# Eight query heads in place of zero-padded ones: 64-row score matmuls in one attention branch

## The reference

```python
C_HEADS, C_KV_HEADS, HEAD_DIM = 8, 2, 64          # branch C: 8 query heads share 2 key/value heads
D_HEADS, D_NOPE, D_ROPE, D_V = 8, 64, 32, 64      # branch D: 8 heads, keys of 64 + 32

def block_attention(q, k, v, scale):              # q (b, l, kv heads, heads per kv head, dk)
    ...
        s = jnp.einsum('bqhgd,bkhd->bhgqk', qblk, k, preferred_element_type=jnp.float32) * scale
        p = jax.nn.softmax(s, axis=-1).astype(v.dtype)
        return jnp.einsum('bhgqk,bkhd->bqhgd', p, v)

def cd_attend(qc, qd, kc, vc, kd, vd, w_out):
    oc = block_attention(qc, kc, vc, HEAD_DIM ** -0.5)
    od = block_attention(qd, kd, vd, (D_NOPE + D_ROPE) ** -0.5)
    return jnp.concatenate([oc, od], axis=-1) @ w_out
```

## Time and profile before

| what | value |
|---|---|
| time, median of 3 runs | 1847.87 us (1847.65 to 1848.35) |
| the profiled execution's own time | 1847.87 us |
| its span in the trace | 1845.5 us |
| mean granted TensorE clock | 0.955 of full speed |
| PE, PEld, DVE, ACT busy | 92%, 76%, 75%, 50% of the span |
| POOL busy | 2.1 us in 6 instructions |
| DMA | 426.38 MB, mean 231 GB/s |

### The profile page before, as it was taken

One profiled execution on the slowest core, in us unless ns is written; L12 is line 12 of the kernel. 1 busy time (PEld: TensorE's weight loads), 2 busy tenths in 40 slices (PEclk: granted clock), 3 DMA queues, 4 the chain that ended last, 5 costly groups with the idle time before them and its releaser, 6 DMA issues.

```text
span 1845.5 us, 22486 instructions
## 1 busy us (share of the span) xinstructions
PE 1693.2 (92%) x8417; PEld 1393.4 (76%) x8418; DVE 1390.7 (75%) x1444; ACT 920.0 (50%) x844; POOL 2.1 (0%) x6
## 2 busy tenths in 40 slices
PE   4988899999999796897799999999899999999995
PEld 1876777888887595566688877888788887888884
DVE  5858757777787827673698977888698977888886
ACT  5421232221221424332577776777677676777773
POOL 0000000000000000000000000000000000000000
PEclk9988999999999798898799999999999999999998
DMA  9543334543675232001499998999899998999992
GB/s 352 190 152 128 117 106 135 178 147 132 208 236 195 64 115 69 23 1 40 141 348 336 360 339 294 347 343 358 279 357 332 359 334 285 352 342 358 336 365 91
DMA packets 214552, 426.38 MB, mean 231 GB/s; under 512 B 8186, under 2 KB 64028, under 8 KB 214452
## 3 DMA queue, kind: packets, MB, share of 16 engines
q1 hardware_dynamic: 210218, 420.37, 65.4%
q10 hardware_dynamic: 4234, 4.57, 0.8%
HBM read 423.86 MB, written 1.05 MB: 230 GB/s over the span
## 4 chain that ended last, share of the span: by engine, by line
PE 87%; DVE 6%; ACT 2%; issue 2%; DMA 1%; SPq 1%; DVEq 0%; ACTq 0%
PE bank L505 26%; PE bank L507 25%; PE bank L506 25%; PE bank L1751 2%; PE bank L1806 2%; DVE lo L464 2%; PE bank L1740 2%; PE bank L1845 1%; PE bank L1526 1%; DMA raw<-in_ada_w_dram 1%; PE bank L1757 1%; PE bank L1520 1%; ACT hi L458 1%; PE bank L1879 0%; PE bank L1880 0%
## 5 line engine op out<-in xcount | busy, mean ns | idle before, releaser
L464 DVE TENSOR_TENSOR lo<-raw,hi 128x2048 fp32r<-128x2048 f32 x361 | 820.7, 2282 | 225.9 <-ACT hi L458 224.2
L458 ACT ACTIVATE hi<-raw 128x2048 fp32r<-128x2048 f32 x361 | 689.1, 1911 | 492.6 <-PE bank L507 471.9
L505 PE MATMUL bank<-hi,xgh 128*128 128x512 f32 (+1 forms) x864 | 331.3, 383 | 24.6 <-issue 18.3
L506 PE MATMUL bank<-lo,xgh 128*128 128x512 f32 (+1 forms) x864 | 327.9, 380 | 0.0
L507 PE MATMUL bank<-hi,xgl 128*128 128x512 f32 (+1 forms) x864 | 327.5, 379 | 0.0
L506 PEld LDWEIGHTS bank<-lo,xgh 128*128 128x128 f32 x864 | 164.4, 190 | 46.7 <-issue 15.0
L505 PEld LDWEIGHTS bank<-hi,xgh 128*128 128x128 f32 x864 | 164.5, 190 | 42.5 <-DVE lo L464 6.5
L507 PEld LDWEIGHTS bank<-hi,xgl 128*128 128x128 f32 x864 | 164.5, 190 | 33.7
L505 PE MATMUL bank<-hi,aTh 128*128 128x512 f32 x396 | 159.1, 402 | 0.0
L507 PE MATMUL bank<-hi,aTl 128*128 128x512 f32 x396 | 154.8, 391 | 0.0
L506 PE MATMUL bank<-lo,aTh 128*128 128x512 f32 x396 | 154.3, 390 | 0.0
(11 more groups left out here) (319 smaller groups left out, 2201.0 us busy)
## 6 DMA issues: line engine op xcount, KB each, us to landing
raw<-in_moe_w_gate_dram SPq DMA_DIRECT2D x99, 1024.0 KB, 6.1
raw<-in_moe_w_up_dram SPq DMA_DIRECT2D x99, 1024.0 KB, 6.5
raw<-in_moe_w_down_dram SPq DMA_DIRECT2D x99, 1024.0 KB, 5.7
raw<-in_ada_w_dram SPq DMA_DIRECT2D x48, 1024.0 KB, 5.8
raw<-in_ffn_w_gate_dram SPq DMA_DIRECT2D x11, 1024.0 KB, 5.4
raw<-in_ffn_w_up_dram SPq DMA_DIRECT2D x11, 1024.0 KB, 5.3
raw<-in_ffn_w_down_dram SPq DMA_DIRECT2D x11, 1024.0 KB, 5.0
raw<-in_ab_w_in_dram SPq DMA_DIRECT2D x6, 1024.0 KB, 8.7
```

The source lines that it names most:

```text
L458: nc.scalar.activation(hi[n0 % SPL][:, 0:size], raw[slot][:, 0:size], ACT.Copy).then_inc(hi_ready, 1)
L464: nc.vector.tensor_tensor(lo[n0 % SPL][:, 0:size], raw[slot][:, 0:size], hi[n0 % SPL][:, 0:size].bitcast(F32), ALU.subtract).then_inc(lo_r ...
L505: nc.tensor.matmul(dst, lh, rh, start=first, stop=False, skip_group_check=True)
L506: nc.tensor.matmul(dst, lh, rl, start=False, stop=False, skip_group_check=True)
```

## The change

The buffer `qcT` becomes a tensor of its own with four planes instead of eight, and nothing in it is set to zero. VectorE copies both halves of a transposed pair of heads at once. A score matmul of branch C takes the 64 partitions of its key head from `qcT` and from `kcT`. GpSimd's block goes, and with it the semaphore `heads_clear` and TensorE's wait on it.

```diff
-        qcT = acc[:].rearrange("p a b (c t) -> p (a b c) t", t=256)
+        qcT = sb("qcT", [P, 4, 256], into=zone2)
...
-        heads_clear = sem("heads_clear")
...
-        @block.gpsimd
-        def _(pool):
-            for cb in (10, 11):
-                full(pool, "ada1", ("bc", cb, 0))
-            nc.gpsimd.memset(qcT[64:128, 0:4, :], 0.0).then_inc(heads_clear, 1)
-            nc.gpsimd.memset(qcT[0:64, 4:8, :], 0.0).then_inc(heads_clear, 1)
...
             for i in range(2):
                 b = full(dve, "heads", ("qc", i))
-                V.tensor_copy(qcT[0:64, 2 * i:2 * i + 2, :], b[0:64, :].rearrange("p (j t) -> p j t", j=2))
-                emptied(V.tensor_copy(qcT[64:128, 4 + 2 * i:6 + 2 * i, :], b[64:128, :].rearrange("p (j t) -> p j t", j=2)),
-                        "heads", ("qc", i))
+                emptied(V.tensor_copy(qcT[:, 2 * i:2 * i + 2, :], b[:].rearrange("p (j t) -> p j t", j=2)), "heads", ("qc", i))
...
-            pe.wait_ge(heads_clear, 2)
...
-                    q_, k_ = (qdT[0:96, h, toks], kdT[0:96, h, :]) if br else (qcT[:, h, toks], kcT[:])
+                    rows = slice(64 * (h // 4), 64 * (h // 4) + 64)
+                    q_, k_ = (qdT[0:96, h, toks], kdT[0:96, h, :]) if br else (qcT[rows, h % 4, toks], kcT[rows, :])
```

## The result

The changed kernel is slower: 1878.88 us (median of 4 runs, 1876.95 to 1879.54) against 1847.76 us for the kernel before, a ratio of 1.0172 with a 95% interval of 1.0154 to 1.0191. 1848.6 was predicted. The profiled execution took 1878.65 us with a span of 1876.4.

What follows compares the result with a forecast made beforehand. TensorE, busy 92%, was taken to bound the kernel, with VectorE's copies on the path ahead of the attention. From 1847.87 us, -1.4 to -0.7 for copies and +1.8 for 13 units gave 1848.6 us, range 1846.8 to 1850.3.

Steps and rivals of the forecast that it cites:

- The clock: Rival: 64-row score matmuls in branch C don't hold 2.4 GHz, 12 units lose 1.63 us each, about 1866 us; chance 0.05.
- The sum: Whole kernel: -1.4 to -0.7 us for copies plus 1.8 for 13 units of branch C, giving 1848.6 us.
- the copies: Ahead of the attention: two VectorE instructions of 0.71 us go, so the first score matmul starts 1.42 us sooner.
- the passages: Branch C's units: 0.09 us per change of row count, making each of 13 units 0.14 us longer, 1.8 us in all.
- the prediction's own signs of being wrong: Branch C: units of 2.33 or 2.6 us or more, clock 0.5 beyond 760 us, or second pass later than 0.43 us.
- what the stages behind do: Output projection, routing and experts, behind the attention: a shift of a few us passes to the end as it is.
- the reserve under VectorE's copy: In a steady unit, the score matmul has streamed 0.09 us before the value matmuls start, hidden under the probabilities' copy.

Runs made afterwards that it cites:

- first128: Changed kernel with branch C's units 0 to 7 over 128 rows and units 8 to 15 over 64 rows; 1844.10 us (one run).
- dfirst: Changed kernel with the branches in the other order, branch D (96 rows) ahead of branch C (64 rows); 1848.12 us, ratio 1.0005 to the kernel before.
- after_warm: Changed kernel with 13 idle matmuls of 128 rows and 512 columns in TensorE's waits ahead of the steady units; 1822.43 us, ratio 0.9871.
- rows66: Changed kernel with 66 rows instead of 64 in each score matmul of branch C; 1873.32 us (one run).
- rows128: Changed kernel with branch C's score matmuls back over all 128 rows and no zeros; 1839.81 us (one run).
- tiny64: Kernel before, with an extra matmul of 64 rows and 2 columns behind each score matmul of branch C; 1831.12 us (one run).

## Why the prediction was wrong

**The step that failed** is the one headed "The clock": "if with half the rows they don't hold the clock at 2.4 GHz", given a chance of 0.05 and kept out of the range. The sum ran all of branch C from 759.40 us on at 1.00 and priced the clock at nothing; in its place the runs showed units 3 to 15 at 0.50 to their end, 61.7 us where they had taken 31.9. The cause named there was the right one, and the argument against it was the mistake: L1510 and L1511 use 4 of 128 columns and brought the clock up. That row says nothing on rows. I noted the difference ("but that is columns, not rows") and let it count all the same.

**What "hold" should have been.** The rival asked whether 64-row units hold the clock. They did, in first128, dfirst and after_warm. They didn't raise it, in any execution of the changed kernel. The earlier trace rows showed that the kernel before enters the steady units at 0.51 and is raised within them, at 759.4, so the question that mattered was what raises it. The forecast took that rise as given ("from 759.40 at 1.00"), although the change alters exactly what TensorE does up to there.

**Its price was too low.** 12 x 1.63 us gave 1866. The unit of 3.96 us in the earlier trace rows was not wholly at the low clock. Units wholly at the low clock take 4.16 us without passages (rows66) and 4.75 with them: 12 x (4.75 - 2.33) = 29.0. For the 13 units from unit 3 on, of the 29.8 us measured, about 13 x (4.75 - 4.16) = 7.7 are passages at the low clock and the other 22 the clock by itself.

**Right: the copies.** 1.42 us were predicted; kdT's copy starts 1.48 sooner and the first score matmul 1.58. Right also that 64 rows don't make a matmul cheaper.

**Right in kind, small in size: the passages.** 0.14 us a unit were predicted for the full clock and 0.20 measured (first128, dfirst), so 13 x 0.20 = 2.6 in place of 1.8. The records of dfirst show which term was short, in duration ns min/median/max of the 64-row units (two records each):

```profile
L1729 PE MATMUL bank<-kcT,qcT x32: 589/641/693, 788.4 to 826.9; 64*128 64x512 f32 x32
```

A passage costs 0.10 us on the way in (the score matmul starts 0.54 us behind the transposes, before 0.44) and 0.09 on the way out (the value matmuls start 0.52 us behind the second record, whose pass is 0.43), as the earlier trace rows had it. But the first record of each score matmul, whose load isn't hidden, takes 693 ns where 595 is usual, and the second starts 0.53 us behind it and not 0.43, one of the prediction's own signs of being wrong: 0.10 for such a load, where 0.05 was taken. So 0.10 + 0.10 + 0.09 - 0.09 = 0.20. The rule of the Trainium skill (TensorEngine Tiling (Array Packing), Key Properties) that a change of tiling mode drains the TensorE agrees with the cost of a changed row count, 0.20 us a unit at the full clock and 0.59 at the low one; where the columns alone changed, had none. With the clock up, the change would have been about the "same" that was forecast: dfirst, which has the change whole and the clock up for branch C, stands at 1.0005, though with its first branch D units at the low clock until 766 us.

**Wrong: what the stages behind do.** They were to pass the shift on as it is; they added 2.7 us, 1.6 of it between the attention and the experts, at a clock of 0.73 against 0.77. That stage isn't steady from run to run: from the last value matmul to the first expert it is 73.1 us in the kernel before and 74.7 in the changed one, and 71.7 to 76.0, at clocks of 0.81 to 0.71, over the twelve kernels of this document. So 1.6 us are no more than its scatter, and not shown to be the change's.

## What to carry to other kernels

Before shrinking the rows of a matmul, look at the granted clock where it stands: if TensorE enters the stretch at the low level, the matmuls that are to be shrunk may be what raises it. Here the padding with zeros cost TensorE nothing and kept the unit at 2.33 us instead of 4.75. Where matmuls of few rows are wanted, put fuller ones ahead of them (first128, dfirst), or fill the waits ahead with matmuls that nobody reads (after_warm). And price a half clock from a stretch that lies wholly in it.

## What else the runs showed

How long the clock stays low under the same busy TensorE differs much. Counted from where TensorE no longer paused, units with 128 rows were at 1.00 after 4.0 us (rows128), 6.4 (the kernel before) and 9.2 (tiny64). Units with 96 rows took 17.5 us in dfirst, 6.3 behind the 66-row units of rows66 and 1.9 behind the 64-row ones of the changed kernel. Those with 66 and 64 rows never were, in 54 and 62 us of steady units (rows66 and the changed kernel). TensorE was busy throughout in all of these, so the busy share doesn't tell them apart. Why 96 rows took so different times stays open, and what lies between 66 and 96 rows wasn't run.

The two passages of a unit cost more at the low clock, 0.59 against 0.20 us. By the working of the prediction 0.09 us of the difference is the reserve under VectorE's copy, which there is at the full clock alone: at the low one the score step of 1.71 us is longer than the copy by itself.

Each turn of the expert loop held TensorE up by 6.0 to 6.4 us in the kernel before, and 13 or 16 extra matmuls ahead of the loop took 22 us off that stage. That is more than anything in the attention gave, and its cause is open.
